# A transformer layer in split fp32: GpSimd makes two of the four weight sums of the seven-product tiles, in a loop of its own

## The reference, cut to what matters

```
def swiglu(x, w_gate, w_up, w_down):
    return (jax.nn.silu(x @ w_gate) * (x @ w_up)) @ w_down
```

## Time and profile before

| | |
|---|---|
| median of three runs | 1111.28 us |
| the profiled execution, its own time | 1110.65 us |
| its span, first to last instruction | 1108.5 us |
| TensorE busy | 1099.8 us (99%) |
| VectorE busy | 775.1 us (70%) |
| ScalarE busy | 534.5 us (48%) |
| GpSimd busy | 34.5 us (3%) |
| mean granted TensorE clock | 0.999 of full |

### The profile page before, as it was taken

How to read it: one execution, slowest core, us unless ns; L and a number is a source line. 1 busy time by engine, 2 the same in 40 slices (tenths; PEclk the granted TensorE clock), 3 DMA queues, 4 the chain that set the end, 5 groups by cost and what they waited for, 6 DMA issues and landing times.

```text
span 1108.5 us, 17958 instructions
## 1 busy us (share of the span) xinstructions
PE 1099.8 (99%) x6752; PEld 975.9 (88%) x6752; DVE 775.1 (70%) x1274; ACT 534.5 (48%) x921; POOL 34.5 (3%) x50
## 2 busy tenths in 40 slices
PE   9999999999999999999999999999999999999997
PEld 7899999988888888888898888889899999998886
DVE  6899999843348588764894865547899999963326
ACT  7455555632325577543463454445355555552222
POOL 0100000000002011010000000000000000000000
PEclk9999999999999999999999999999999999999999
DMA  6543333353313123242253252131233333363302
GB/s 228 191 116 113 115 115 114 124 185 97 95 59 112 58 87 86 96 152 79 73 165 121 84 164 77 52 120 58 76 115 115 115 105 108 114 193 110 96 19 76
DMA packets 33593, 121.27 MB, mean 109 GB/s; under 512 B 3900, under 2 KB 3916, under 8 KB 33264
## 3 DMA queue, kind: packets, MB, share of 16 engines
q1 hardware_dynamic: 30528, 109.07, 31.3%
q0 software_dynamic: 2992, 11.19, 3.1%
HBM read 118.13 MB, written 2.11 MB: 108 GB/s over the span
## 4 chain that ended last, share of the span: by engine, by line
PE 99%; DVE 0%; DMA 0%; ACT 0%; issue 0%; DVEq 0%
PE ps L530 20%; PE ps L532 20%; PE ps L531 20%; PE ps L610 10%; PE ps L608 10%; PE ps L609 10%; PE ps L832 1%; PE ps L547 1%; PE ps L811 1%; PE ps L899 1%; PE ps L883 1%; PE ps L804 0%; PE ps L803 0%; DMA raw<-in_units 0%; PE ps L995 0%; PE ps L756 0%
## 5 line engine op out<-in xcount | busy, mean ns | idle before, releaser
L1600 DVE TENSOR_TENSOR wlo<-raw,whi 128x1024 fp32r<-128x1024 f32 x124 | 152.1, 1232 | 164.0 <-ACT whi L1061 162.9
L1061 ACT ACTIVATE whi<-raw 128x1024 fp32r<-128x1024 f32 (+1 forms) x131 | 134.4, 1032 | 134.8 <-PE ps L532 124.1
L530 PE MATMUL ps<-whi,hhi 128*128 128x512 f32 x480 | 187.8, 391 | 0.0
L532 PE MATMUL ps<-whi,hlo 128*128 128x512 f32 x480 | 186.9, 389 | 0.0
L531 PE MATMUL ps<-wlo,hhi 128*128 128x512 f32 x480 | 186.8, 389 | 0.0
L530 PE MATMUL ps<-xth,whi 128*128 128x512 f32 (+1 forms) x340 | 130.2, 383 | 0.0
L532 PE MATMUL ps<-xth,wlo 128*128 128x512 f32 (+1 forms) x340 | 128.1, 377 | 0.0
L531 PE MATMUL ps<-xtl,whi 128*128 128x512 f32 (+1 forms) x340 | 128.0, 376 | 0.0
L532 PEld LDWEIGHTS ps<-whi,hlo 128*128 128x128 f32 x480 | 90.1, 188 | 18.9
L530 PEld LDWEIGHTS ps<-whi,hhi 128*128 128x128 f32 x480 | 90.1, 188 | 18.3 <-ACT km L1061 0.3
L531 PEld LDWEIGHTS ps<-wlo,hhi 128*128 128x128 f32 x480 | 90.1, 188 | 18.3
(11 more groups left out here) (258 smaller groups left out, 2657.3 us busy)
## 6 DMA issues: line engine op xcount, KB each, us to landing
raw<-in_units SPq DMA_DIRECT2D x204, 512.0 KB, 3.6
xn<-in_x POOLq DMA_DIRECT2D x4, 512.0 KB, 7.7
gb<-in_ln_g POOLq DMA_DIRECT2D x4, 512.0 KB, 3.8
gb<-in_ln_b POOLq DMA_DIRECT2D x4, 512.0 KB, 5.3
wb<-in_bias_by_key POOLq DMA_DIRECT2D x8, 256.0 KB, 3.0
out<-xn SPq DMA_DIRECT2D x8, 256.0 KB, 2.1
gsp<-g_rows POOLq DMA_DIRECT2D x1, 1024.0 KB, 4.9
memn<-in_mem_cols POOLq DMA_DIRECT2D x1, 1024.0 KB, 6.9
```

The costliest lines, as they stand in the source:

```text
L530: mm(dst, lh, rh, start=start, stop=False)
L532: return mm(dst, ll, rh, start=False, stop=stop)
L1061: return nc.scalar.activation(*a, **k)
L1600: v.tensor_tensor(wlo[c % SPL][:, :], raw[c % RAW][:, :], whi[c % SPL][:, :].bitcast(F32), ALU.subtract).then_inc(lo_done, 1)
```

## The change: two of the four sums move to GpSimd

GpSimd gets a loop, `first_sums(n)`, which makes t0 and t1 of tiles 4 to 21 of FFN n. For each tile it waits until both raw units have landed and until `tsum[n]` is free, makes the two sums and counts each in a new semaphore, `pool_sums`. `first_sums(0)` stands behind the four loads of x, `first_sums(1)` behind `load_gb(2)`. VectorE waits for `pool_sums` where it made those two sums before, and makes t2 and t3 as before. ScalarE's high part of t0,t1 waits for `pool_sums`; `sums_done` now counts one per tile.

```
+            def first_sums(n):
+                t = tsum[n]
+                for f in range(FAST0, FT):
+                    c = U_FFN[n] + 2 * f
+                    g, u = raw[c % RAW], raw[(c + 1) % RAW]
+                    pool.wait_ge(raw_in[c % RAW], 16 * (c // RAW + 1))
+                    pool.wait_ge(raw_in[(c + 1) % RAW], 16 * ((c + 1) // RAW + 1))
+                    if n and f == FAST0:
+                        pool.wait_ge(xlo_done, NB * 3)
+                    elif f > FAST0:
+                        pool.wait_ge(sums_lo_done, 2 * fast_count(n, f) - 2)
+                    nc.gpsimd.tensor_tensor(t[:, 0, :], g[:, 0:512], u[:, 0:512], ALU.add).then_inc(pool_sums, 1)
+                    nc.gpsimd.tensor_tensor(t[:, 1, :], u[:, 512:], u[:, 0:512], ALU.add).then_inc(pool_sums, 1)
...
             for b in range(NB):
                 pool.dma_start(xn[:, b, :], x[0, b * P:(b + 1) * P, :]).then_inc(x_in[b], 16)
+            first_sums(0)
             pool.wait_ge(small_in, 16 * SMALL)
...
             load_gb(2)
+            first_sums(1)
             pool.wait_ge(unit_used, U_F2 + 2 * FT)
...
                 def sums(j):
-                    act.wait_ge(sums_done, 2 * q - 1 + j)
+                    act.wait_ge(sums_done, q) if j else act.wait_ge(pool_sums, 2 * q)
...
-                if f > FAST0:
-                    dve.wait_ge(sums_lo_done, 2 * fast_count(n, f) - 2)
-                step.inc(v.tensor_tensor(t[:, 0, :], g[:, 0:512], u[:, 0:512], ALU.add))
-                v.tensor_tensor(t[:, 1, :], u[:, 512:], u[:, 0:512], ALU.add).then_inc(sums_done, 1)
-                dve.wait_ge(v_step, step.base + step.k)
+                dve.wait_ge(pool_sums, 2 * fast_count(n, f))
                 step.link(v.tensor_tensor(t[:, 2, :], t[:, 0, :], u[:, 512:], ALU.add))
                 v.tensor_tensor(t[:, 3, :], t[:, 2, :], g[:, 512:], ALU.add).then_inc(sums_done, 1)
```

More of the change, by code:

```diff
@@ L380, in macaron_layer @@
         sums_done = sem("sums_done")
+        pool_sums = sem("pool_sums")
         sums_hi_done = sem("sums_hi_done")
```

## The result

The changed kernel takes 1115.30 us (median of five runs, 1113.29 to 1116.36), the kernel before on the same chip 1111.28 us (1110.69 to 1112.53): ratio 1.0033, 95% interval 1.0023 to 1.0044. That is 4.0 us slower by the medians, and the spread has grown from 1.8 to 3.1 us. The profiled execution is the fastest of the five: 1113.29 us, span 1111.5 us, against 1110.65 and 1108.5 before. So the profile shows 2.6 to 3.0 us of the loss, and some 1.4 us of the median lies in executions that it doesn't show.

What follows compares the result with a forecast made beforehand. TensorE, busy 1099.8 of 1108.5 us, was taken to bound the kernel. A 2.3 us stall at the first FFN's first seven-product tile and 0 elsewhere took the median from 1111.28 to 1113.6 us, range 1111.3 to 1117.5.

Steps and rivals of the forecast that it cites:

- What bounds the kernel: Whole kernel: TensorE bounds it, busy 1099.8 of 1108.5 us; taking 50 us off VectorE buys nothing by itself.
- First FFN, first tile: Tile 4: GpSimd's sums start late behind nine DMA issues, so TensorE stalls 2.3 us before product 7.
- The next tiles: Tiles right after tile 4, first FFN: 0 to 0.3 us more TensorE loss, taken as 0.
- Middle tiles: Middle tiles cost nothing: GpSimd starts as `lo_last` ends; loop 9.35 us against TensorE's 9.56, margin 0.21 us.
- Second FFN: Second FFN costs nothing: GpSimd has both sums of tile 4 ready more than 10 us early.
- The sum: Whole kernel: 2.3 us at the first tile; profiled execution 1110.65 to 1112.95 us, median 1113.6 us.
- 0 elsewhere: All places other than the first FFN's first seven-product tile: no added time, 0 us.
- mild form: Rival: tile loop makes VectorE fall back 0.1 us a tile, about 1115 us; chance 0.11 together with the strong form.
- The clock's rival: Rival: granted clock falls behind TensorE's first-tile stall, some 2 to 4 us more, 1116 to 1118 us; chance 0.03.
- GpSimd free later than its rows show: Rival: GpSimd still writes descriptors after 44.23 us; with 3 us, 1116.6 us; chance 0.12, shared with u(5) landing much later.
- The loop too long: Rival: tile loop exceeds TensorE's period, 9.85 us, VectorE falling back 0.3 us a tile; about 1121.7 us; chance 0.11, both forms.
- Given back later: Rival: TensorE's 2.3 us loss at tile 4 is recovered at later waits, giving 1111.3 us; chance 0.08.

Runs made afterwards that it cites:

- E2: Changed kernel with GpSimd's loop in the second FFN alone, VectorE making all four sums in the first; ratio 0.9995 to the kernel before, 1110.62 us.
- E4: Changed kernel with GpSimd's two sums of tile 4, first FFN, in front of its wait and nine DMA issues; ratio 0.9998 to the kernel before, 1111.04 us.
- E1: Changed kernel with all four sums of tile 4, first FFN, back on VectorE; GpSimd keeps the other 35 tiles; ratio 1.0000 to the kernel before, 1111.38 us.
- E3: Changed kernel with GpSimd's loop in the first FFN alone; ratio 1.0040 to the kernel before, 1115.61 us.
- E6: Changed kernel with one extra GpSimd add, waited for, ahead of tile 4's sums in the first FFN; ratio 1.0045 to the kernel before, median 1116.60 us.
- E11: Changed kernel with a third GpSimd add, waited for, ahead of t0 in each of the 36 tiles; ratio 1.0316 to the kernel before, 1146.47 us.
- E5: Changed kernel run again, unaltered; ratio 1.0041 to the kernel before, 1114.36 to 1117.34 us.
- E10: E9 with TensorE's wait before product 7 of tile 4 filled by 16 unused matmuls; ratio 1.0038 to the kernel before, median 1114.71 us.
- E9: Changed kernel with x's loads moved behind tiles 12 to 18, two adds holding GpSimd up as long; ratio 1.0039 to the kernel before, median 1116.10 us.
- E7: Changed kernel with 16 unused matmuls just ahead of TensorE's wait for product 7 of tile 4, first FFN; ratio 1.0035 to the kernel before, median 1115.21 us.

## Why the prediction was right or wrong

**What bounds the kernel**: right. The work taken off VectorE bought nothing in any version; the best, E2 and E4, equal the kernel before. It was less than the 50 us of the prediction, which counted 0.69 us for each sum although they stand 0.6 us apart: VectorE's busy time fell from 775.1 to 738.5 us, by 36.6. Nothing in the sum hangs on it.

**First FFN, first tile**: right in place, order and size. The chain GpSimd's DMA issues, t0 and t1, `lo_both`, load of u(5), landing, t0 and t1 of tile 5, ScalarE, `copy6`, product 7 is what the trace shows, every time in it within 0.3 us of the forecast. TensorE loses 2.06 us there in the profiled execution, where the sum had 2.3. The term that was too large is the landing: 3.5 us, not 3.9. E1, E3 and E4 show the cause: with these two sums back on VectorE or in front of the DMA issues the loss goes, and with the loop in the first FFN alone it is all there. E6, later still, has a longer wait in its profile, but no median that tells.

**The next tiles**: 0.13 us between 60 and 72 us, inside the 0 to 0.3 given and taken as 0.

**Middle tiles**: cost nothing, as forecast, but GpSimd's start is set by another thing than the step said. It was to start as `lo_last` ends; in 32 of its 36 tiles it waits for a landing instead, and in most it starts 0.1 to 0.4 us before `lo_last` (line 1696) ends:

```profile
107.77 1.52 POOL L468 TENSOR_TENSOR tsum<-raw,raw 128x512 f32<-128x512 f32 x1 [6.25 <-DMA raw<-in_units]
109.24 1.30 POOL L469 TENSOR_TENSOR tsum<-raw 128x512 f32<-128x512 f32 x1
...
107.44 0.69 DVE L1696 TENSOR_TENSOR sel<-raw,seh 128x512 fp32r<-128x512 f32 x1
...
110.67 0.69 DVE L1678 TENSOR_TENSOR tsum<-tsum,raw 128x512 f32<-128x512 f32 x1 [1.54 <-POOL tsum L469]
```

The add that began beside `lo_last` took 0.22 us longer (1.52 against 1.30). The third sum before this one stood at 101.65, so the loop is 9.02 us and not 9.35; the margin to 9.56 is 0.5 us, more than twice the 0.21 forecast. The hand-over was 0.13 us (109.24 + 1.30 to 110.67), where I took 0.24. E11 shows that a loop above the period does cost.

**Second FFN**: right (E2).

**The sum**: here it went wrong in size. For its own execution the forecast was 1112.95 us and 1113.29 was measured; for the median it was 1113.6 and 1115.3 came. The step that failed is the one from the profiled execution to the median: "0 elsewhere" and 0.63 us between the two, as before. It took the loss to be one number that carries over from execution to execution; the profiled execution now stands 2.0 us below the median. The wait that the change opens has two things attached to it that vary. One is the landing of u(5), 3.5 to 5.1 us, which before was hidden by 1.4 us of room at `copy6(4)` and now goes straight to TensorE: side by side with the kernel before, TensorE loses 2.1 us at that place with a landing of 3.5 us, 3.2 with 4.7 (E5) and 3.4 with 5.1 (E10). The other is the rival that had 0.03: the clock falls behind the wait, for 1.6 us (E3, E5, E9). The bounds that the prediction gave for the landing, 3.3 to 7.6 us, hold all of these; the sum took one value of them. The clock's rival had argued from 0.5 us of idling; idling of 1.8 us and more is another matter. It was priced at 2 to 4 us, which no row gave; 1.6 was measured. The two together don't account for every execution (below). That 1115.3 us lies in the range is in part luck: its upper part was drawn for a later GpSimd and for a mild form of the loop, and neither came. The rest of the profiled loss is 0.17 us in the first ten us, where the kernels are the same, and 0.67 us at 437 us (below).

**The other rivals**: GpSimd free later than its rows show is refuted: its first add starts at 44.41, 0.01 us after the last DMA issue ends. That agrees with what the Trainium skill (Perfetto Trace Analysis, "DMA Instruction — SWDGE (GPSIMD)") says of that end, as the prediction cites it. The loop too long is refuted for this kernel and shown for E11; its mild form had about 1115 us, near the median measured, but TensorE waits in no middle tile. Given back later is refuted: over the 1040 us that follow, less than 0.2 us in all is given back.

**What stays open**: what makes u(5) land late in some executions; loads of x are not needed for it (E10). How much of the median is clock and how much is landing: filling the wait lowered the median by 0.9 and 1.4 us (E7 against E5, E10 against E9), in the direction and near the size of the clock's 1.6, but the intervals overlap. What carries executions at full clock up to 1116.7 us: the latest landing in a profile, 5.1 us, gave 1114.58 us, and the other 2 us stand in no profile. A landing later still would do it, and is not shown. Two executions with the same wait of 1.8 us, one with the fall and one without, are not explained either.

## What to carry to other kernels

Moving work to an idle engine is judged by that engine's queue at the first use, not by its busy share: GpSimd was 3% busy and some 5 us late, because nine DMA issues stood ahead of the first sum. When an engine at 99% is made to wait even once, count what hangs on that wait as well: the spread of every transfer that was hidden before, and a fall of the clock behind it. Take the profile of several executions, since one may be the fastest of its kernel and show two thirds of the loss, as here.

## What the runs showed of the hardware

- The granted clock went to half behind a wait of TensorE of 1.8 us in one execution (E9) and not in another (changed kernel), and came back after 3.4 us; in E6, with 3.6 us of waiting, it went down within the wait and came back after 6.8 us. With the wait filled by matmuls it stayed full in both profiles (E7, E10). At the lower level matmuls of 256 columns started every 0.21 instead of 0.114 us.
- The 0.67 us at 437 us in the profile after has nothing to do with the FFNs. One of GpSimd's bias adds, which come when their masks land, met a VectorE instruction with one SBUF input and an SBUF output, 128x128, which took 1.10 us instead of the 0.29 us it takes at other places:

```profile
436.70 1.28 POOL L506 TENSOR_TENSOR wb<-wb,lnm_sb 128x512 f32<-128x512 f32 x1 [3.35 <-DMA wb<-in_bias_by_key]
436.96 1.10 DVE L1969 TENSOR_SCALAR lg<-lg,rinv 128x128 f32<-128x128 f32 x1
```

  TensorE waited for it (the 0.3 us for `lg` in the waits above). In the kernel before, the same instruction came 1.06 us after the start of the add instead of 0.26, and took 0.32 us. So, by this one meeting, it isn't only VectorE instructions with two SBUF inputs that meet GpSimd's adds: a short one with a scalar operand is held as well, until the add is over (436.70 + 1.28 = 437.98, where VectorE goes on at 437.98). The Trainium skill (SBUF — State Buffer, "Who interferes with whom") names this kind too, and this row agrees.
